# Four half rows of the expert gather, moved from between the last dense dots to behind the third ring item

## The reference, cut to what matters

```python
def block(tb):                       # 128 tokens, 2 blocks
    q = (tb @ w_query).reshape(tbn, 8, 128)
    # top 16 of 128 keys on each half, then top 16 of the 256 pairs, per head
    top_s, pos = lax.top_k(cand, 16)
    idx = jnp.take_along_axis(cand_idx, pos, axis=-1)
    gate = jax.nn.softmax(top_s, axis=-1)
    u = expert_u[idx]                # 128 rows of 2048 per token
    v = expert_v[idx]
    act = jax.nn.gelu(jnp.einsum('td,thkd->thk', tb, u))
    return jnp.einsum('thk,thkd->td', gate * act, v)
```

## Time and profile before

| | us |
|---|---|
| median of 3 runs (lowest, highest) | 1838.11 (1835.63, 1841.41) |
| the profiled execution, its own time | 1832.72 |
| its span, first to last instruction | 1830.9 |
| mean granted TensorE clock | 0.886 of full |
| busy: PE, DVE, ACT, POOL | 1457.1, 1311.3, 435.1, 891.4 |
| moved by DMA | 683.72 MB, mean 373 GB/s |

### The profile page before, as it was taken

One profiled execution on the slowest core, in us unless ns is written; L12 is line 12 of the kernel. 1 busy time (PEld: TensorE's weight loads), 2 busy tenths in 40 slices (PEclk: granted clock), 3 DMA queues, 4 the chain that ended last, 5 costly groups with the idle time before them and its releaser, 6 DMA issues.

```text
span 1830.9 us, 13641 instructions
## 1 busy us (share of the span) xinstructions
PE 1457.1 (80%) x4521; PEld 707.6 (39%) x4521; DVE 1311.3 (72%) x1684; ACT 435.1 (24%) x1160; POOL 891.4 (49%) x666
## 2 busy tenths in 40 slices
PE   5999999999999556655655666669999999989920
PEld 3434564575459312111111233345444444433300
DVE  3128877676138999999998787898556556556699
ACT  3012211120122222121223586687100000000000
POOL 0012233211006788888777787756455554322273
PEclk9999999999999766666667898979999999999965
DMA  9999989796658999999999999979999999999997
GB/s 364 378 361 342 352 334 326 300 348 244 221 186 345 380 418 420 418 418 420 419 419 417 405 406 391 381 291 386 414 413 412 413 413 413 381 418 417 417 422 312
DMA packets 164022, 683.72 MB, mean 373 GB/s; under 512 B 16433, under 2 KB 19057, under 8 KB 120689
## 3 DMA queue, kind: packets, MB, share of 16 engines
q0 software_dynamic: 92160, 503.36, 68.4%
q1 hardware_dynamic: 71360, 176.36, 25.5%
q10 hardware_dynamic: 432, 3.15, 0.4%
HBM read 678.51 MB, written 4.29 MB: 373 GB/s over the span
## 4 chain that ended last, share of the span: by engine, by line
DMA 35%; PE 28%; POOL 16%; DVE 14%; issue 5%; SPq 2%; ACT 0%; DVEq 0%; POOLq 0%; ACTq 0%
DMA arena<-in_expert_v,arena 27%; POOL arena L568 16%; DMA arena<-in_expert_u,arena 6%; PE PS L1807 6%; PE PS L1666 6%; PE PS L1567 5%; DVE arena L1382 5%; DVE arena L1425 3%; PE PS L1883 2%; DVE arena L1417 2%; PE PS L1548 2%; SPq L384 1%; PE PS L1523 1%; DMA arena<-in_w_mod 1%; DMA arena<-in_w_in 1%
## 5 line engine op out<-in xcount | busy, mean ns | idle before, releaser
L1382 DVE CUSTOM_DVE_ANT_0 arena<-arena 128x2048 f32<-128x2048 f32 x256 | 578.4, 2288 | 95.4 <-DMA arena<-in_expert_u,arena 94.4
L1883 PE MATMUL PS<-arena 128*128 128x512 f32 x512 | 364.1, 851 | 242.1 <-DMA arena<-in_expert_v,arena 242.0
L568 POOL DMA_INDIRECT arena<-in_expert_v,arena x256 | 401.9, 1570 | 285.8 <-DVE arena L1425 108.7
L568 POOL DMA_INDIRECT arena<-in_expert_u,arena x256 | 393.0, 1535 | 257.6 <-DVE arena L1357 89.5
L1935 PE MATMUL PS<-arena 128*128 128x512 f32 x1024 | 452.9, 600 | 16.3 <-DMA arena<-in_expert_v 14.2
L1935 PEld LDWEIGHTS PS<-arena 128*128 128x128 f32 x1024 | 192.7, 191 | 275.8 <-issue 227.4
L1883 PEld LDWEIGHTS PS<-arena 128*128 128x128 f32 x512 | 117.0, 253 | 456.4 <-DMA arena<-in_expert_v,arena 359.7
L1425 DVE SCALAR_TENSOR_TENSOR arena<-arena 128x2048 f32<-128x2048 f32 x62 | 145.8, 2351 | 56.9 <-DMA arena<-in_expert_v,arena 54.5
L1098 DVE SCALAR_TENSOR_TENSOR arena<-arena 128x1024 f32<-128x1024 f32 x120 | 160.9, 1341 | 25.7 <-DMA arena<-in_w_mod 22.9
L498 POOL DMA_DIRECT2D arena<-in_w_mod x128 | 68.8, 539 | 211.4 <-DVE arena L1098 180.7
L952 ACT ACTIVATE arena<-arena 128x4 f32<-128x4 f32 x64 | 13.0, 203 | 587.3 <-DVE arena L1382 516.2
(11 more groups left out here) (247 smaller groups left out, 1330.5 us busy)
## 6 DMA issues: line engine op xcount, KB each, us to landing
arena<-in_w_mod POOLq DMA_DIRECT2D x128, 512.0 KB, 7.3
arena<-in_expert_v SPq DMA_DIRECT2D x128, 512.0 KB, 8.0
arena<-in_w_mod SPq DMA_DIRECT2D x32, 1024.0 KB, 14.3
arena<-in_w_in SPq DMA_DIRECT2D x28, 1024.0 KB, 14.4
arena<-in_w_out SPq DMA_DIRECT2D x16, 1024.0 KB, 12.9
arena<-in_w_query SPq DMA_DIRECT2D x8, 1024.0 KB, 8.5
arena<-in_x SPq DMA_DIRECT2D x4, 1024.0 KB, 6.1
arena<-cum_rows SPq DMA_DIRECT2D x4, 1024.0 KB, 10.0
```

What stands on the lines that cost most here:

```text
L568: nc.gpsimd.indirect_dma_start(slot, None, table, bass.IndirectOffsetOnAxis(ap=rows[:, n:n + 1], axis=0),).then_inc(arrived, 16)
L1382: V.tensor_tensor_reduce(out=rows, in0=rows, in1=h2row[u // PH], scale=1.0, scalar=0.0, op0=ALU.mult, op1=ALU.add, accum_out=dots[:, u % B ...
L1883: ins = M(PS[:, b, :], diag_slot[m % DIAGS], slot[:, b * NQ:(b + 1) * NQ], start=(m == 0), stop=(m == BLK - 1))
```

## The change

Rows 112 to 115 get the positions 198 to 201. Nothing in the program of DVE changes. On POOL their four gathers are issued behind ring item 2. On PE their products come behind the last `scatter` of block 0 (n = 197) and ahead of `coef_transpose_stacked`. On ACT their diagonals move into the last dense group (dots 188 to 191), behind the doubled copy of the coefficients.

```diff
-V_POS = [20 + 110 * m // 62 if m < 62 else 130 + 57 * (m - 62) // 50 for m in range(V_EARLY)] + [187, 188, 190, 191]
+V_POS = [20 + 110 * m // 62 if m < 62 else 130 + 57 * (m - 62) // 50 for m in range(V_EARLY)] + [198, 199, 200, 201]
...
             for k in range(3):
                 item_load(k)
+            for m in range(V_EARLY, V_LATE):
+                gather_v(m)
             for m in range(V_LATE, BLK):
                 gather_v(m)
                 item_load(m - V_LATE + 3)
```

## The result

| | before | changed |
|---|---|---|
| first comparison, median of 8 runs | 1839.15 | 1846.97 |
| ratio, first comparison | | 1.0066 (1.0044 to 1.0088) |
| ratio, second comparison (10 runs of the same file) | | 1.0028 (1.0015 to 1.0041) |
| span of the profiled execution | 1830.9 | 1845.1 |
| first route selection of the experts (L1352, L1354 after) | 554.8 | 562.5 |

The account below looks back on a forecast made before the run. It took DMA transfers as the bound, delayed by whatever delays dots 192 and 193. Terms: 0 for DVE's lost wait, +7.5 us for the hold, 0 for the landing; median 1838.1 to 1845.6 us, range 1838.5 to 1850.0.

Parts of the forecast that it names:

- The hold: Four products ahead of PE's transpose delay L1406 on DVE, hence dot 193 and item 4's transfers, by 7.5 us.
- DVE's 3.67 us: DVE's wait for a late scatter product, in front of L1396, was to go; credited as 0 in the sum.
- POOL's wait: POOL's single 12.84 us idle time before item 3 was to split into two waits.
- the second stop: Transfers were to stop twice, so that the stretch without any is some 14 us in all.
- ACT's last group: Last gate products on ACT for block 0, forecast to start at 1217.0 instead of 1219.02.
- The rows: Four row products on PE behind the last scatter: 10.1 us, bounds 7.9 and 13.8, ending at 1228.95.
- Item 3: POOL's ring item 3, behind row 116's gather, goes near 1223.8, 1.1 us later than before, at no cost.
- The landing: The four gathered half rows, issued beside dots 188 to 191, land before PE wants them; cost nothing.
- Rival 1: After item 4, transfers recover up to 5.5 us of the hold: +2.0, 1840.1; chance 0.16.
- Rival 2: PE's clock is high when the rows begin, four at 1.98 us: +5.3, 1843.4; chance 0.10.
- Rival 3: Faster: PE enters double products at the high clock, ring and clock as in rivals 1 and 2: -3.0, 1835.1; chance 0.09.
- The ends of the range: Whole-kernel range from 1838.5, taking in rival 1, to 1850.0, the upper bound of the hold.

Follow-up runs that it names:

- products only: Kernel before with products and diagonals moved as in the change, the four gathers left where they stood; ratio 1.0027, 652.8 us from last selection to end.
- the transpose first: Changed kernel with the coefficient transpose ahead of the four products instead of behind them; ratio 0.9986, 647.7 us from last selection to end.
- six rows: Changed kernel with six rows (110 to 115) instead of four behind the last scatter; ratio 1.0058, 655.4 us from last selection to end.
- the last version: Changed kernel, transpose before the products, dots 192 to 194 before first halves 32, 33 and L1406, items 3 and 4 before row 116's gather; ratio 0.9991, 643.2 us.
- filler: Changed kernel plus 20 unused unit-matrix products on PE, 14 behind scatter 28 and 6 behind scatter 30; ratio 1.0044, 651.8 us from last selection to end.

## Why the prediction was right, and where it was not

**The hold: right as a mechanism, and in size by some luck.** I had +7.5 us; the traces give 7.75 for the whole cost, and for L1406 8.4 in the first pair of profiles and 7.0 in the second. DVE's 3.67 us went, POOL's wait split in two, the second stop came, PE waited for no data in front of the four rows, as listed. The stops came out shorter than the 14 us without any transfer that I had listed: 7 us at 43 GB/s and 3 us at 55.

**ACT's last group: mis-sized.** "The last group starts at 1217.0" meant 2 us sooner than before (1219.02). That is +31.0; it started at +33.1 and +32.5 in the two changed profiles and +32.4 in products only, against +33.0 and +33.4 before, so it gained about 0.5 us. The pair of scatters 29 and 30 now took 3.76 us at the low clock while ACT waited for them (idle 1.74 us there), which I had left out; before, three of them ran right behind row 115 in 2.96 us. And the profile I read had the gate group two before the last unusually early (+11.3, where every other kernel that keeps rows 110 and 111 in place has +12.4 to +13.3).

**The rows: nearly.** 10.1 us foreseen, 9.09, 8.65 and 9.17 measured; transpose and copies 0.9 foreseen, 0.6 measured. ACT's group was 2.1 and 1.5 us later than foreseen, the rows 1.0 and 1.45 shorter, the copies 0.3: L1406 came at +44.7 and +43.6, where +43.85 was foreseen. That two wrong terms of 1 to 2 us cancel is luck.

**Item 3: later than foreseen.** I had it 1.1 us later than before; it went at +40.2 instead of +36.7, 3.6 us later, since row 112 was done later. It cost nothing beside a hold of 8.3 us, as written.

**The landing, the gathers beside dots: right.** The four gathers took 2.51, 2.37, 1.91 and 1.91 us beside the dots, the last ended at +29.8 and no row waited for its data; products only, where they were issued early, cost the same.

**Rival 1, the catching up: no.** From item 4 to the end it is 603.9 and 604.4 us before, 603.8 and 604.7 changed, 604.1 with products only. In these five profiles a hold of item 4 is passed on whole. It is not a rule for every order: with the transpose first the same stretch is 601.9 us, with six rows 605.9, in the last version 609.0.

**Rival 2, the high clock from the first row: no.** The granted clock was 0.50 from 1224 to 1231 and 1.00 from 1231 on, so only the later rows had it, and the four took 9.09 us and not 7.9.

**Rival 3, faster: no, though its first half came.** PE entered the double products at the high clock, 1.68 and 1.98 us instead of 3.06 and 3.44, but as written against it PE was not what DVE waited for: the time from item 4 to the end did not change.

**The ends of the range: the step that failed.** I wrote that the end shifts by 7.5 and let the range end at 1850.0, "the upper bound of the hold", as if nothing but the hold could differ between the two kernels in a comparison. The first comparison's ratio of 1.0066 on 1838.1 is 1850.2, 12 us, and its interval begins at 8.1; the second's is 5.1 us. I had read a spread of 5.8 us in three runs and put it in the chances (0.3%), but gave it no term in the ends of the range. What the runs show in its place: 7.1 us of difference in the first 560 us between two executions of one and the same program, nearly as much as the whole cost of the change (7.75 us). The first comparison is itself uneven: its medians differ by 7.8 us, its means by 10.6, since two of the eight changed runs (1857.54 and 1859.77) lie 8 us and more above the next (1849.11). What makes executions differ so was not tried, and why this comparison gives 12 us stays open.

## What to carry to other kernels

When work is moved off a wait, look at what stands behind it in its new place, on the same engine, and follow that to the transfers: here one transpose behind four products held a vector instruction, that held a dot, and that held the ring's next transfers. Ask for each of these links whether the order is needed; two of them (the transpose behind the products, the dot behind L1406) could be cut by a change of order alone, and each cut by itself gave back 5.4 and 5.75 of the 7.75 us. And measure a change of some us also in the traces, by the time from the last instruction that it can't touch, with each kernel traced twice, and not by the medians alone.

## What was not expected of the hardware

Two executions of one program differed by 7.1 us at the first route selection (554.8 and 561.9) and by 0.8 us in the 645 us that follow the last one; over all kernels here the first selection lies between 554.8 and 570.0. And where matmuls were moved away, those that stayed took longer: three scatter products in 2.96 us before, two (29 and 30) in 3.76 after. PE had been idle for 6.04 us in front of these, and the granted clock was 0.50 from 1218 to 1224 us; with a filler that left 2.99 us of idle time in front of them they took 3.29.
